# The third column pair of each FFN as seven products, token tiles copied to y by ScalarE, and keys loaded one stream further ahead

## The reference

```
def macaron_half(x, g_pre, g_post, w_in, w_out):
    return x + 0.5 * rms_norm(swiglu(rms_norm(x, g_pre), w_in, w_out), g_post)

def swiglu(h, w_in, w_out):          # w_in 1024 x 5632, w_out 2816 x 1024
    gate, up = jnp.split(h @ w_in, 2, axis=-1)
    return (jax.nn.silu(gate) * up) @ w_out
```

## Time and profile before

| | |
|---|---|
| Median of 3 runs | 2545.0 us (2541.86 to 2545.66) |
| Profiled execution, own time | 2546.58 us |
| its span, first to last instruction | 2544.8 us |
| mean granted TensorE clock | 0.993 |
| first products in summed form | 4 x (8 + 11) = 76 pairs |

### The profile page before, as it was taken

The page is one execution under the profiler, slowest core; times in us unless marked ns, Lnnn a source line. Parts: engine busy times, 40 slices in busy tenths (PEclk is TensorE's granted clock), DMA queues, the critical chain, the costliest instruction groups (busy, mean ns, idle before and its releaser), DMA issues. The chain is left out here.

```text
span 2544.8 us, 46214 instructions
## 1 busy us (share of the span) xinstructions
PE 2466.8 (97%) x18529; PEld 2247.2 (88%) x18529; DVE 1499.4 (59%) x2111; ACT 1081.7 (43%) x1896; POOL 111.7 (4%) x104
## 2 busy tenths in 40 slices
PE   8999999999879999999999999999999999999998
PEld 7998998999658876998899899899989779988997
DVE  7744765433646756874575687367462468745754
ACT  5532543222645654452354445235342444523542
POOL 0000001000102221000000100000010010000001
PEclk9999999999999999999999999999999999999999
DMA  4232323222470004232233432222323122322332
GB/s 133 83 95 63 88 80 129 66 75 88 153 225 20 3 13 124 84 91 71 78 88 107 136 92 74 87 79 83 128 86 98 62 95 88 91 71 79 84 110 104
DMA packets 285465, 229.40 MB, mean 90 GB/s; under 512 B 24924, under 2 KB 237046, under 8 KB 285320
## 3 DMA queue, kind: packets, MB, share of 16 engines
q1 hardware_dynamic: 285320, 227.38, 29.7%
HBM read 212.43 MB, written 14.91 MB: 89 GB/s over the span
## 5 line engine op out<-in xcount | busy, mean ns | idle before, releaser
L544 PE MATMUL ps<-row_hi,hid_hi 128*128 128x512 f32 x880 | 345.5, 393 | 0.0
L544 PE MATMUL ps<-row_hi,hid_lo 128*128 128x512 f32 x880 | 344.6, 392 | 0.0
L544 PE MATMUL ps<-row_lo,hid_hi 128*128 128x512 f32 x880 | 344.4, 391 | 0.0
L485 DVE TENSOR_TENSOR row_lo<-row_raw,row_hi 128x512 fp32r<-128x512 f32 x200 | 141.3, 719 | 268.1 <-ACT row_hi L477 267.9
L477 ACT ACTIVATE row_hi<-row_raw 128x512 fp32r<-128x512 f32 x200 | 124.1, 629 | 409.7 <-DMA row_raw<-in_ffn_w_out_dram 218.6
L544 PEld LDWEIGHTS ps<-row_lo,hid_hi 128*128 128x128 f32 x880 | 165.2, 188 | 36.9
L544 PEld LDWEIGHTS ps<-row_hi,hid_hi 128*128 128x128 f32 x880 | 165.1, 188 | 36.1
L544 PEld LDWEIGHTS ps<-row_hi,hid_lo 128*128 128x128 f32 x880 | 165.1, 188 | 36.0
L736 PE MATMUL ps<-t_hi,pair_hi 128*128 128x320 f32 x608 | 188.1, 309 | 3.4 <-DVE hid L1017 3.4
L736 PE MATMUL ps<-act_lo,pair_hi 128*128 128x320 f32 x608 | 188.0, 309 | 0.0
L736 PE MATMUL ps<-t_lo,pair_hi 128*128 128x320 f32 x608 | 188.0, 309 | 0.0
(11 more groups left out here) (449 smaller groups left out, 5722.5 us busy)
## 6 DMA issues: line engine op xcount, KB each, us to landing
pair_raw<-in_ffn_w_in_dram SPq DMA_DIRECT2D x104, 512.0 KB, 5.1
row_raw<-in_ffn_w_out_dram SPq DMA_DIRECT2D x160, 256.0 KB, 3.0
ring_raw<-in_ffn_w_in_dram SPq DMA_DIRECT2D x72, 512.0 KB, 5.2
pair_raw<-in_even_w_in_dram SPq DMA_DIRECT2D x22, 512.0 KB, 3.8
x_memory<-x SPq DMA_DIRECT2D x15, 512.0 KB, 2.6
x<-x_memory SPq DMA_DIRECT2D x15, 512.0 KB, 4.2
norm_buf<-in_norm_g_dram SPq DMA_DIRECT2D x12, 512.0 KB, 5.5
x<-in_x_prompt_dram SPq DMA_DIRECT2D x8, 512.0 KB, 4.8
```

The source lines that it names most:

```text
L485: dve.tensor_tensor(row_lo[n][:, :], raw, row_hi[n][:, :].bitcast(F32), ALU.subtract).then_inc(s_row_lo, 1)
L544: mm = pe.matmul(ps[:, bank, :], a[:, k, t * P:(t + 1) * P], w[n][:, :], start=(k == 0 and w is row_hi and a is left_hi), stop=(k == kt - ...
```

## The change

- SUMMED_FROM becomes (2, 0): the third pair of the first chunk of each FFN is summed too, 4 x (9 + 11) = 80 pairs.
- y gets the turned normed tokens by a copy from PSUM by ScalarE (`act_copied`), tile by tile, in the order (t k a c) instead of (k t a c). In the first FFN GpSimd writes tiles 0 to 2 instead, as act_hi + act_lo (`pool_tokens`). `dve_high_tokens` is gone.
- TensorE waits for the copies before it overwrites their banks: turns of tiles 2 and 4, and the first pair.
- VectorE takes two of the four token differences before the first pair's work and two inside it. The four low parts are spread over the second pair's tile, between the weights' work for the summed pair. TensorE waits for each token sum where it needs it.
- SP issues keys b+1 ahead of values b; the eight state loads go, two at a time, behind values 3 to 6.

```diff
-        SUMMED_FROM = (3, 0)
+        SUMMED_FROM = (2, 0)
...
+        def pool_tokens(pool):
+            for t in range(3):
+                cols = slice(t * P, (t + 1) * P)
+                pool.wait_ge(s_alo, t + 1)
+                pool.tensor_tensor(y[:, t, :].rearrange("p (k c) -> p k c", c=P), act_hi[:, :, cols].bitcast(F32),
+                                   act_lo[:, :, cols].bitcast(F32), ALU.add).then_inc(s_copied, 1)
...
             after_first(pe, s_joined, q, 3, 2)
+            token_sum(1)
             product(E_BANK, of_sum((s12_hi, s12_lo), 0), of_sum(first), True).then_inc(s_prod, 1)
             pe.wait_ge(s_moved, q * 4 + 1)
+            token_sum(2)
             product(B_BANK, of_sum((s12_hi, s12_lo), 1), of_sum(second), False).then_inc(s_prod, 1)
             product(A_BANK, of_pair(0, 1), half(1, 0), False).then_inc(s_pair_mm[0], 1)
             pe.wait_ge(s_pair_lo[1], n + 2)
             pe.wait_ge(s_moved, q * 4 + 3)
+            token_sum(3)
             product(B_BANK, of_pair(1, 0), of_sum(third), False).then_inc(s_prod, 1)
...
             pe.wait_ge(s_joined, q * 3 + 1)
+            token_sum(4)
             product(B_BANK, of_pair(1, 1), of_sum(fourth), False).then_inc(s_pair_mm[1], 1)
...
+                    if f:
+                        pe.wait_ge(s_copied, 5 * f + 2)
                     pe_first_pair(pe, n0, m)
                     for j in range(1, p):
                         pe_pair(pe, n0 + j)
-                    pe.wait_ge(s_tlo, 4 * (f + 1))
...
# act_ffn, the tile before the first summed one
                     if summed:
+                        act_hi0(act, 0, n0 + p, raw_of(f, 0, 0)[1])
                         act_hi12(act, k0)
-                        act_hi0(act, 0, n0 + p, raw_of(f, 0, 0)[1])
-                        act_hi4(act, k0)
...
# act_ffn, first summed tile, between its copies
+                    if c == 0 and isinstance(j, int) and j == p:
+                        act_hi2(act, 0, n0 + p, k0)
+                        act_hi4(act, k0)
...
# dve_ffn, the tile before the first summed one
                     if summed:
+                        dve_token_low(dve, f, 0)
                         dve_sums(dve, 0, k0, raw_of(f, 0, 0)[1])
+                        dve_lo_pair(dve, 0, 0, n0 + p)
                         dve_lo12(dve, k0)
-                        dve_lo_pair(dve, 0, 0, n0 + p)
-                        dve_sum4(dve, 0, k0)
-                        dve_lo4(dve, k0)
                     else:
                         dve_split_pair(dve, 0, n0 + j + 1)
+                    if c == 0 and j == 0:
+                        for i in range(2, 4):
+                            dve_token_sum(dve, f, i)
                     dve.wait_ge(s_pair_mm[1], n0 + j + 2)
...
-                    beside_tokens = c == 0 and j == 1
-                    if beside_tokens:
-                        dve_token_low(dve, f, 1)
+                    if summed:
+                        dve_sum4(dve, 0, k0)
+                        dve_token_low(dve, f, 2)
                     dve.wait_ge(s_hid_hi, hb + j + 1)
...
-                    if beside_tokens:
-                        dve_token_low(dve, f, 2)
                     if summed:
+                        dve_token_low(dve, f, 1)
                         dve_lo_pair(dve, 0, 1, n0 + p)
+                        dve_lo4(dve, k0)
+                        dve_token_low(dve, f, 3)
                     else:
                         dve_split_pair(dve, 1, n0 + j + 1)
-                    if beside_tokens:
-                        dve_token_low(dve, f, 3)
...
                 if c == 0:
-                    dve_high_tokens(dve, f)
+                    for i in range(2):
+                        dve_token_sum(dve, f, i)
                     tile(0, FFN_NORM[f])
-                    dve_token_sums(dve, f)
-                    dve_token_low(dve, f, 0)
...
+        def act_copied(act, m, t):
+            act.wait_ge(s_alo, 5 * m + t + 1)
+            if m:
+                act.wait_ge(s_xnew, 5 * (m - 1) + t + 1)
+            b = TURN_BANKS[t]
+            act.activation(y[:, t, :], ps[:, b:b + 2, :].rearrange("p a c -> p (a c)"), ACT.Copy).then_inc(s_copied, 1)
...
# act_norm (act_first_norm gets copies 3 and 4 at its end)
+                if m in FFN_NORM and s == TT - 1:
+                    act_copied(act, m, 1)
+                    act_copied(act, m, 2)
                 if m < NORMS:
                     act_root_ahead(act, m, s)
+                if m in FFN_NORM and s == 2:
+                    act_copied(act, m, 0)
             if m < NORMS:
                 act_turned(act, m, 3)
                 act_turned(act, m, 4)
+            if m in FFN_NORM:
+                act_copied(act, m, 3)
+                act_copied(act, m, 4)
...
+            if m in FFN_NORM and m and t in (2, 4):
+                pe.wait_ge(s_copied, 5 * FFN_NORM.index(m) + t - 1)
...
+            keys(0)
+            values(0)
+            sp.wait_ge(s_bs, PSTEPS)
+            keys(1)
+            sp.wait_ge(s_bs, 2 * PSTEPS)
+            values(1)
+            keys(2)
+            sp_rwkv_loads(sp)
+            for b in range(2, NSEQ):
+                if b + 1 < NSEQ:
+                    keys(b + 1)
+                values(b)
+                if 3 <= b < 7:
+                    sp_state_loads(sp, b - 3)
```

More of the change, by code:

```diff
@@ L775, in pe_ffn @@
                         pe_pair(pe, n0 + j)
-                    pe.wait_ge(s_tlo, 4 * (f + 1))
-                pe_summed(pe, n0 + p, k0)
+                pe_summed(pe, n0 + p, k0, f if c == 0 else None)
                 with pe.Fori(0, FF_K - p - 1) as i:
@@ L845, in tile @@
                     act.activation(halves(hid_hi, j), hid[:, :, :], ACT.Copy).then_inc(s_hid_hi, 1)
-                    if summed:
-                        act_hi2(act, 0, n0 + p, k0)
-                    else:
+                    if not summed:
                         act_split_pair(act, 1, n0 + j + 1)
@@ L940, in dve_lo_pair, with dve_token_sum @@
                               pair_hi[half][:, :, :].bitcast(F32), ALU.subtract).then_inc(s_pair_lo[half], 1)
[L942 to L949, removed]
-            b1, b2 = token_rows(0), token_rows(1)
[L951 to L958, removed]
-            dve.tensor_tensor(b2[:, :, :, 0, :], b2[:, :, :, 0, :], b2[:, :, :, 1, :], ALU.subtract).then_inc(s_tsum, 1)
+        def dve_token_sum(dve, f, i):
+            b1, b2 = token_rows(0), token_rows(1)
+            out, left, right = ((b1[:, :, :, 0, :], b1[:, :, :, 1, :], b1[:, :, :, 0, :]),
+                                (b1[:, :, :, 1, :], b2[:, :, :, 1, :], b1[:, :, :, 1, :]),
+                                (b2[:, :, :, 1, :], b2[:, :, :, 1, :], b1[:, :, :, 0, :]),
+                                (b2[:, :, :, 0, :], b2[:, :, :, 0, :], b2[:, :, :, 1, :]))[i]
+            dve.wait_ge(s_copied, 5 * (f + 1))
+            if i:
+                dve.wait_ge(s_tsum, 4 * f + i)
+            dve.tensor_tensor(out, left, right, ALU.subtract).then_inc(s_tsum, 1)
         def dve_token_low(dve, f, i):
@@ L1137, in act_first_norm @@
             act_turned(act, 0, 4)
+            act_copied(act, 0, 3)
+            act_copied(act, 0, 4)
         def act_norm(act, m, scale, groups):
@@ L1701, in sp_streams, with keys, values @@
             sp.dma_start(new_mask, io["new_mask"].rearrange("p (b c) -> p b c", c=P)).then_inc(s_att_const, 16)
-            for b in range(NSEQ):
-                slot = b % 2
-                if b == 1:
-                    sp.wait_ge(s_bs, PSTEPS)
-                if b == 2:
-                    sp_rwkv_loads(sp)
+            def keys(b):
                 if b >= 2:
                     sp.wait_ge(s_tk, 2 * (b - 1))
-                sp.dma_start(k_cache[slot], io["cache_fox_k"][0, b].rearrange("(t p) h d -> p t (h d)", p=P))\
-                  .then_inc(s_kc[slot], 16)
-                if b == 1:
-                    sp.wait_ge(s_bs, 2 * PSTEPS)
+                sp.dma_start(k_cache[b % 2], io["cache_fox_k"][0, b].rearrange("(t p) h d -> p t (h d)", p=P))\
+                  .then_inc(s_kc[b % 2], 16)
+            def values(b):
                 if b >= 2:
                     sp.wait_ge(s_o2, b - 1)
-                sp.dma_start(v_cache[slot], io["cache_fox_v"][0, b].rearrange("(t p) h d -> p t (h d)", p=P))\
-                  .then_inc(s_vc[slot], 16)
+                sp.dma_start(v_cache[b % 2], io["cache_fox_v"][0, b].rearrange("(t p) h d -> p t (h d)", p=P))\
+                  .then_inc(s_vc[b % 2], 16)
+            keys(0)
[12 more added lines that the diff above has]
+                    sp_state_loads(sp, b - 3)
         def pe_streams(pe, step):
@@ L2022, in sp_rwkv_loads, with sp_state_loads @@
             sp.dma_start(lora_g[:, :], io["rw_g2"][0]).then_inc(s_rwc, 16)
-            for j in range(4):
-                for h in range(2):
```

(6 more changed lines are left out.)

16 lines of the change are left out of this document (10 added, 6 removed).

## The result

The changed kernel took 2561.64 us, median of 6 runs (2557.43 to 2570.37), beside 2543.84 for the kernel before in the same comparison (6 runs): ratio 1.0082, 95% interval 1.0068 to 1.0097, slower. The forecast was 2552.8 with a range of 2539 to 2561. The profiled execution took 2562.45 (span 2560.6), 15.9 more than that of before. Its mean granted clock is 0.989, against 0.993.

A forecast was written before the change was run, and what follows sets the result against it. The prediction took TensorE, in flight for 97% of the span, as the bound, through its matmul count and waits. Its terms, -7.0 + 12.8 + 5.0 + 2 - 5.0 = +7.8 us, gave 2552.8 us, range 2539 to 2561.

The forecast's parts named there:

- Seven products: Third pair as seven products: twelve matmuls fewer in each of four FFNs, -7.0 us, called certain.
- Joined add: First summed pair of each FFN's first chunk: TensorE stalls 3.2 us for VectorE's add, four times, +12.8 us.
- First-pair wait: Start of the last three FFNs: TensorE waits about 3.3 us for ScalarE's copy to y, together +5.0 us net.
- No wait of 0.7 for pair_lo: Sign: TensorE's old 0.71 us wait for the second pair's low part in each of the last three FFNs goes.
- GpSimd's adds: First norm: GpSimd's three adds in the first FFN hold up VectorE's scalings, +2 us, bounds 0 to 4.
- Keys: Streams' stage: keys asked for one stream ahead remove 4.9 us of TensorE waits, -5.0 us, bounds -5.4 to -2.
- The rival that they gain nothing: Streams' stage: DMA is the limit, so +5 on whatever else holds, 2558; counted within the forecast's chance of 0.52.
- the clock falls: Rival: seven new TensorE idle times of about 3 us lower its clock; two falls would give 2561; chance 0.08.
- the prediction's own sentence on the Trainium skill: The skill warns of such gaps repeated between bursts, making a clock fall likelier than the one 2.5 us row suggests.

The follow-up runs named there:

- before_copies: The kernel before plus only the two late ScalarE token copies to y and TensorE's wait for them before the first pair in three FFNs: 2551.5 us, 1.0038.
- pool_late: The changed kernel with GpSimd's three token adds of the first FFN held back until the first norm's scalings are done: 2554.69 us, one run.
- keys_only: The kernel before with only the new order of key, value and state loads: 2537.79 us, 0.9981.
- low_early: The changed kernel with two token subtractions moved ahead of VectorE's wait for the second pair's last product: 2558.88 us, 1.0067.
- mended_more: The changed kernel with token tile 1's copy, one subtraction, act_hi2 and first summed tile's joined add earlier, GpSimd's adds after the first norm's scalings: 2533.92 us, 0.9971.
- fill_first: The changed kernel with 15 matmuls that nobody reads run in TensorE's wait ahead of the first pair of three FFNs: 2553.11 us, 1.0048.
- fill_join: The changed kernel with 20 matmuls that nobody reads run ahead of the wait for the first joined add in four FFNs: 2552.57 us, 1.0045.

## Why the prediction was too low, step by step

- *Seven products, −7.0*: 48 matmuls fewer. Its price was not run alone. The first FFN bears it out, where the clock stands at 1.00 in both profiles: from the start of the second pair to the rows' loop it takes 126.7 us before and 128.2 after, +1.5, where the forecast for this stretch is −1.8 + 3.2 = +1.4.
- *Joined add, 3.2 each*: 15.1 − 3.4 = 11.7 over four, 2.9 each, for the reason given. VectorE's timeline is the one that was added up.
- *First-pair wait, about 3.3 and +5.0 net*: 3.3 each, behind the root of the last tile. before_copies prices it at 7.1 with the old waits of 0.7 still in, 5.0 without them.
- *No wait of 0.7 for pair_lo*: gone.
- *GpSimd's adds, +2*: +1.3, and pool_late gives 1.1 of it back.
- *Keys, −5.0*: the waits fell by 4.9 − 0.8 = 4.1, keys_only measures −4.1. The rival that they gain nothing is refuted.
- These make −7.0 + 11.7 + 5.0 + 1.3 − 4.1 = +6.9, for a forecast of +7.8. The remainder says +4.8 to +6.8. The program was forecast rightly; three terms were about 1 us off each, and one of these errors offsets another.

*The step that failed is the clock.* The sum had no term for it, that is, it priced it at nothing, and the rival "the clock falls" got a chance of 0.08. The runs show 13 to 17 us there. The reason for the nothing was one row: behind an idle time of 2.5 us the clock stood at 1.00. The same trace of the kernel before has the opposite, 200 us earlier, behind an idle time of 2.86 us:
```profile
774.72 1.86 PE L2269 MATMUL ps<-ident,norm_buf 64*64 64x64 f32 x29 [2.86 <-DVE norm_buf L2705]
```
```profile
775.00:780.00 5.00, 5.00 (x72) 4.67 (x71) 1.52 (x3) 1.12 (x2) 2.24 (x2) 0.50 0.00 0
```
It has another behind 2.55 us at 2075.99. So the trace could have told that a wait of 3 us is no safe place, and the prediction's own sentence on the Trainium skill leaned that way too; the chance stayed at 0.08. The chosen row itself was a chance. In the changed kernel's profile the same stage, with an idle time of 2.68 us at the same instruction, shows the clock lower:
```profile
976.42 1.09 PE L2553 MATMUL ps<-rw,xn_buf 64*64 64x256 f32 x16 [2.68 <-DVE streams_state L2883]
```
```profile
970.00:980.00 10.00, 7.32 (x69) 5.80 (x66) 5.08 (x8) 3.03 (x6) 0.00 (x0) 0.88 0.70 207
```
pool_late has 0.83 there behind 2.33 us. All fourteen profiles together give a price. The wait of 2.86 us stands in each of them, between 768 and 785 us, and in each the clock falls in it or behind it. At the FFNs' starts nine of them have bare waits of 3.0 to 3.3 us, 42 in all. The clock falls at 38 of these, and the average over the 42 is 2.0 us lost. (A fall is counted when it begins between 0.5 us before the wait and 2 us after it.) Seven such waits make 14 us, an estimate from these profiles that fits the 13 to 17 of the runs. The rival had the right mechanism but named 2561 for two falls of up to 4 us; the profile has six, of 1.7 or 3.4 us each.

That the idle times themselves bring this, and not something else in the change, rests above all on the fillings. They leave the operands as late as they were and give TensorE work in the wait, the falls vanish just where the filling is, and the clock's part is 6.5 and 11.6 us less. before_copies adds three such waits to the kernel before; its profile has falls behind two of them, though its times alone don't show the clock's part clear of noise. The Trainium skill ("TensorE: Matmul & The Clock Gate", "HAM oscillation — how this bites in real kernels") tells of a kernel in which TensorE waits about 3 to 5 us for a DMA between bursts of matmuls and runs at the lower clock after each such wait. The waits here, 3.0 and 3.3 us, stand at the lower end of that, and 38 of 42 agree with it. The rule of thumb at the head of the same section would have let waits of this length pass; here the measurement decides against it.

A second miss was in an experiment: low_early was expected to work by a count of VectorE alone. ScalarE's queue order, which the change had fitted to the old VectorE order, took the gain.

Open: why two fillings are worth no more than one; and what decides whether the clock falls at waits below 2.8 us. Falls there come and go between executions, and not all stand behind a long wait: in the kernel before's profile one begins at 937.9 behind three waits of 0.6 to 0.8 us.

## What to carry to other kernels

On an engine that is busy 97% of the time, count new idle times as well as their sum: one of 3 us cost 3 us and, on average, 2 more of clock. Before pricing a new gap, look at every gap of that length that the old trace has, not at one: a gap that doesn't bring the clock down in one profile may do so in the next run. Take the granted clock of all runs, and split each span by it before explaining the program. Where a change is all in order and still slower, look for instructions that stand in an in-order queue ahead of the one that is awaited and are needed later: a few such moves, on three engines, turned +0.8% into −0.3%, of which 0.2% is the new order of loads.

## What the runs showed of the hardware that was not expected

- TensorE's granted clock fell from 2.4 to 1.2 GHz behind 38 of 42 waits of 3.0 to 3.3 us, and at all fourteen of 2.86 us (one in each profile). A fall at the FFNs' starts lost 1.7 or 3.4 us (0.83 or 0.66 of a 10 us window). Behind waits of 1.3 us at the first pairs, and 0.7 to 1.0 at the add, mended_more's profile shows none. Short waits are not always safe: in before's profile the clock fell at 2006 behind one of 1.23 us that had one of 0.5 us close ahead of it.
- Runs of one kernel spread by the clock: over the kernel before's 57 runs it was 0.991 to 0.997, and the span followed it with a correlation of 0.88.
- Matmuls whose result nobody reads, placed in a wait, made the changed kernel 8.5 us (fill_first) and 9 us (fill_join) faster.
- A VectorE scaling with SBUF operands took 3.21 us beside GpSimd adds and 1.28 alone; a subtraction 1.53 instead of 1.22. The two GpSimd adds took 5.67 us together there; the third took 2.39.
